# Dilated attention in a fused transformer kernel: the product with the values turned round, so that it leaves the array by features

## What is computed

```python
q, k, v = split(x @ w_in, 3)               # 48 heads of 64: 3 patterns x 16 heads
q, k = rope(rmsnorm(q)), rope(rmsnorm(k))
for g, (window, dilation) in enumerate(((128, 1), (512, 4), (2048, 16))):
    o[g], lse[g] = banded_softmax_attention(q[g], k[g], v[g])
wts = softmax(stack(lse), axis=0)          # over the three patterns
y = sum_g(wts[g] * o[g]) @ w_out           # 16 heads of 64 -> 1024
```

## Time and profile before

| | us |
|---|---|
| median of 3 runs (2498.86 to 2504.4) | 2503.65 |
| the profiled execution's own time | 2499.47 |
| its span | 2498.2 |
| PE busy (share of the span) | 2326.4 (93%) |
| DVE busy | 1221.8 (49%) |
| ACT busy | 969.2 (39%) |
| mean granted PE clock, share of full | 0.961 |

### The profile page before, as it was taken

The page is one execution under the profiler, slowest core; times in us unless marked ns, Lnnn a source line. Parts: engine busy times, 40 slices in busy tenths (PEclk is TensorE's granted clock), DMA queues, the critical chain, the costliest instruction groups (busy, mean ns, idle before and its releaser), DMA issues.

```text
span 2498.2 us, 37765 instructions
## 1 busy us (share of the span) xinstructions
PE 2326.4 (93%) x16663; PEld 2120.0 (85%) x16663; DVE 1221.8 (49%) x1521; ACT 969.2 (39%) x1145; POOL 506.6 (20%) x453
## 2 busy tenths in 40 slices
PE   6999999989999999889999899979999989888998
PEld 6998899979999998557999877867888877657997
DVE  5645566646555543445655345362122264545444
ACT  3433344434343433334444244333222233534442
POOL 2112434302111211220221101012202210230220
PEclk9999999989999999789999999989999999999999
DMA  6555433445555555666554310113332322213551
GB/s 242 175 173 173 139 122 133 136 169 174 182 179 185 180 182 173 229 237 236 172 183 155 124 35 18 34 68 101 101 98 88 102 96 85 68 51 93 181 183 68
DMA packets 205245, 344.72 MB, mean 138 GB/s; under 512 B 8845, under 2 KB 69498, under 8 KB 205082
## 3 DMA queue, kind: packets, MB, share of 16 engines
q1 hardware_dynamic: 205082, 342.31, 41.0%
HBM read 341.24 MB, written 1.05 MB: 137 GB/s over the span
## 4 chain that ended last, share of the span: by engine, by line
PE 80%; DVE 9%; POOL 4%; ACT 4%; issue 2%; SPq 0%; DMA 0%; DVEq 0%; POOLq 0%; ACTq 0%
PE PS L466 77%; PE PS L475 3%; DVE WL L452 2%; ACT WH L439 1%; POOL small L1454 1%; DVE rstd L587 1%; DVE XL L634 1%; POOL TMP L1463 1%; DVE XL L1002 0%; DVE al L998 0%; POOL small L1452 0%; DVE TMP L1382 0%; POOL TMP L1464 0%; DVE TMP L1387 0%; DVE al L1371 0%
## 5 line engine op out<-in xcount | busy, mean ns | idle before, releaser
L452 DVE TENSOR_TENSOR WL<-raw,WH 128x2048 fp32r<-128x2048 f32 (+2 forms) x281 | 651.6, 2331 | 720.7 <-ACT WH L439 720.7
L466 PE MATMUL PS<-XH,WH 128*128 128x256 f32 (+1 forms) x2336 | 699.3, 299 | 40.3 <-issue 15.3
L466 PE MATMUL PS<-XL,WH 128*128 128x256 f32 (+1 forms) x2336 | 692.9, 297 | 0.0
L466 PE MATMUL PS<-XH,WL 128*128 128x256 f32 (+1 forms) x2336 | 692.6, 297 | 0.0
L439 ACT ACTIVATE WH<-raw 128x2048 fp32r<-128x2048 f32 (+2 forms) x281 | 518.8, 1858 | 361.6 <-PE PS L466 361.1
L466 PEld LDWEIGHTS PS<-XH,WH 128*128 128x128 f32 x2336 | 451.6, 193 | 56.6 <-issue 18.5
L466 PEld LDWEIGHTS PS<-XL,WH 128*128 128x128 f32 x2336 | 452.6, 194 | 10.1
L466 PEld LDWEIGHTS PS<-XH,WL 128*128 128x128 f32 x2336 | 452.2, 194 | 10.0
L466 PE MATMUL PS<-WH,XH 128*128 128x256 f32 (+2 forms) x944 | 287.3, 304 | 17.3 <-DVE XL L634 8.5
L466 PE MATMUL PS<-WL,XH 128*128 128x256 f32 (+2 forms) x944 | 279.1, 296 | 0.0
L466 PE MATMUL PS<-WH,XL 128*128 128x256 f32 (+2 forms) x944 | 278.9, 295 | 0.0
(11 more groups left out here) (232 smaller groups left out, 2573.2 us busy)
## 6 DMA issues: line engine op xcount, KB each, us to landing
raw<-in_ffn_w_in SPq DMA_DIRECT2D x88, 1024.0 KB, 5.1
raw<-in_w_mod SPq DMA_DIRECT2D x48, 1024.0 KB, 5.2
raw<-in_ffn_w_out SPq DMA_DIRECT2D x40, 1024.0 KB, 4.9
raw<-in_a_w_in SPq DMA_DIRECT2D x36, 1024.0 KB, 4.9
raw<-in_w_mlp_in SPq DMA_DIRECT2D x32, 1024.0 KB, 5.5
raw<-in_w_mlp_out SPq DMA_DIRECT2D x32, 1024.0 KB, 5.0
raw<-in_gla_w_in SPq DMA_DIRECT2D x12, 1024.0 KB, 5.0
raw<-in_attn_w_qkv SPq DMA_DIRECT2D x6, 1024.0 KB, 5.0
```

The lines of the kernel that those rows point to most:

```text
L452: dve.e.tensor_tensor(self.WL[j % NRAW][:, 0:nk * nn], self.raw[j % NRAW][:, 0:nk * nn], wh.bitcast(F32), ALU.subtract).then_inc(*self.lo. ...
L466: return self.pe.e.matmul(out, l, r, start=start, stop=stop, skip_group_check=skip)
```

## The change

`pv` now takes two steps (the two heads of a pair, same token block) at once. The weights are 64 columns of values, in the left half of the array's columns for one head and in the right half for the other, their matmuls in turns, and what moves is the 128 columns of `aPT`. So bank 7 holds features on its partitions and tokens along the row. Both steps are done at even i. `turn_p` uses bank 5 or 6 for the first block only, and bank 3 (second half of an even step), 2 and 4 (odd step) for the rest. The inverse sums are taken at i = 7, behind the rotation, spread by ACT over 64 columns a head at the start of i = 8, and transposed on PE (`sums`, 4 transposes). ACT copies bank 7 out at the end of a group, and DVE multiplies the copy with the transposed inverses. The result is already by features: `turn_o` goes, and the split into `XH` and `XL` is done in four parts, three of them in group 3 at i = 1, 3, 5 and one at the end.

```diff
@@ attn_out_pe / attn_out_act / attn_out_dve
-        self.turn_o_pe(tag + "o", O, ready, 1)
+        if O is not None:
+            self.turn_o_pe(tag + "o", O, ready, 1)
...
-        self.turn_o_act(tag + "o", 1)
+        if tag == "lat":
+            self.turn_o_act(tag + "o", 1)
@@ new, per part g of the output
+        self.act.e.activation(self.XH[h][:, 2 * g:2 * g + 2, :], O, ACT.Copy).then_inc(*self.xh.up((tag, 2 * g)))
...
+        self.dve.e.tensor_tensor(self.XL[h][:, 2 * g:2 * g + 2, :], O, self.XH[h][:, 2 * g:2 * g + 2, :].bitcast(F32), ALU.subtract).then_inc(*self.xl.up((tag, 2 * g)))
@@ dilated_pe, turn_p
-                b = spare = 11 - spare
+                if u or c0:
+                    b = ((None, 3), (2, 4))[u][c0 // 3]
+                else:
+                    b = spare = 11 - spare
@@ dilated_pe, pv(hs, s0)
+            for s in (s0, s0 + 1):
                 pe.wait_ge(self.emptied, ("dil", "p", hs, s))
...
+                for s in (s0, s0 + 1):
+                    pair, j = divmod(hd, 2)
+                    m = self.mm(PS[64 * j:64 * j + 64, 7, pair * 256 + tb * 128:pair * 256 + tb * 128 + 128], self.aV[hb][:, g, kb * 256 + hd * 64:kb * 256 + hd * 64 + 64],
+                                self.aPT[s % 2][:, i * 128:i * 128 + 128], i == 0, i == 3 * nk - 1, True)
@@ dilated_pe
+        def sums(hs):
+            b = spare = 11 - spare
+            pe.wait_ge(self.evac, ("dil", "r", hs))
+            self.pe_bank(b)
...
+                    m = self.tr(PS[:, b, o:o + 128], self.aT[3][:, 256 * tb + 128 * pair:256 * tb + 128 * pair + 128])
@@ dilated_pe, main loop
                     turn_p(hs, i - 1)
-                    if i > 1:
-                        pv(hs, i - 2)
                     turn_p(hs, i)
                 if hs >= 0 and i in (2, 4, 6, 8):
                     pv(hs, i - 2)
                 if hs >= 0 and i == 8:
-                    pv(hs, 7)
+                    sums(hs)
@@ dilated_act, main loop
             for i in range(10):
+                if hs >= 0 and i == 8:
+                    act.wait_ge(self.v_step, ("dil", "recip", hs))
+                    act.e.activation(self.aT[3].rearrange("p (h d) -> p h d", d=64), self.small[:, 48:56].unsqueeze(2).to_broadcast([128, 8, 64]), ACT.Copy).then_inc(*self.evac.up(("dil", "r", hs)))
                 if hs + 1 < 4 and i < 9:
                     self.act_begin()
...
+                if hs == 3 and i in (1, 3, 5):
+                    split(i // 2)
+            if hs >= 0:
+                act.wait_ge(self.weighed, ("dil", hs, 7))
+                act.e.activation(self.aOT[:, 2 * hs:2 * hs + 2, :], PS[:, 7, :].rearrange("p (k t) -> p k t", k=2), ACT.Copy).then_inc(*self.evac.up(("dil", "o", hs)))
+        split(3)
@@ dilated_dve, main loop
+                if hs == 3 and i in (1, 3, 5):
+                    self.split_o_dve("dilo", i // 2, 1, self.aOT[:, i - 1:i + 1, :])
+                if hs >= 0 and i == 7:
+                    dve.wait_ge(self.expd, ("dil", hs, 7))
+                    dve.e.reciprocal(rd, den).then_inc(*self.v_step.up(("dil", "recip", hs)))
...
-            dve.wait_ge(self.weighed, ("dil", hs, 7))
-            dve.e.reciprocal(rd, den).then_inc(*self.v_step.up(("dil", "recip", hs)))
...
-                t = dve.e.tensor_tensor(dst[:, tb], PS[:, 7, tb * 256:tb * 256 + 256].rearrange("p (h d) -> p h d", h=4),
-                                        rd[:, 4 * tb:4 * tb + 4].unsqueeze(2).to_broadcast([128, 4, 64]), ALU.mult)
...
+            dve.e.tensor_tensor(self.aOT[:, 2 * hs:2 * hs + 2, :], self.aOT[:, 2 * hs:2 * hs + 2, :], two(PS[:, self.bank_of["dil", "r", hs], :]), ALU.mult).then_inc(*self.o_done.up(("dil", hs)))
```

More of the change, by code:

```diff
@@ L270, in phase_views @@
         self.aO = v(X0, 0, [128, 2048]).rearrange("p (b d) -> p b d", b=2)
+        self.aOT = self.tiles(v(X0, 0, [128, 2048]))
         self.aT = [v(X1, 512 * i, [128, 512]) for i in range(4)]
@@ L963, in x_free @@
         return {"dil": [(self.turned, ("residual", 0, 3)), (self.v_step, "tables")],
-                "f1": [(self.turned, ("dilo", "o", 3))],
+                "f1": [(self.xl, ("dilo", 5))],
                 "f2": [(self.lin, ("f1", "up", 5))],
@@ L1121, in turn_o_dve, with split_o_act, split_o_dve @@
             self.xl.name((tag, 2 * k2 + 1))
+    def split_o_act(self, tag, g, h, O, ready):
+        for signal, key in ready:
+            self.act.wait_ge(signal, key)
+        self.act.e.activation(self.XH[h][:, 2 * g:2 * g + 2, :], O, ACT.Copy).then_inc(*self.xh.up((tag, 2 * g)))
+    def split_o_dve(self, tag, g, h, O):
+        self.dve.wait_ge(self.xh, (tag, 2 * g))
+        self.dve.e.tensor_tensor(self.XL[h][:, 2 * g:2 * g + 2, :], O, self.XH[h][:, 2 * g:2 * g + 2, :].bitcast(F32), ALU.subtract).then_inc(*self.xl.up((tag, 2 * g)))
+        self.xl.name((tag, 2 * g + 1))
     def attn_out_pe(self, tag, O, ready, w_out):
-        self.turn_o_pe(tag + "o", O, ready, 1)
+        if O is not None:
+            self.turn_o_pe(tag + "o", O, ready, 1)
         for half in range(2):
@@ L1135, in attn_out_dve @@
     def attn_out_dve(self, tag, nxt, at):
-        self.turn_o_dve(tag + "o", 1)
+        if tag == "lat":
+            self.turn_o_dve(tag + "o", 1)
         for half in range(2):
@@ L1232, in turn_p, with pv @@
                 self.empties([b], (self.evac if c0 else self.emptied, ("dil", "p", hs, s)))
-        def pv(hs, s):
-            hd, tb, _ = self.dil_step(s)
-            u, hb = s % 2, hs % 2
+        def pv(hs, s0):
+            hb, tb = hs % 2, s0 // 2 % 2
             nk = tb + 1
-            for i in range(3 * nk):
-                o, kb = divmod(i, nk)
-                g = self.dil_order(s)[o]
+            if s0 == 0:
+                self.pe_bank(7)
+            for s in (s0, s0 + 1):
                 pe.wait_ge(self.emptied, ("dil", "p", hs, s))
@@ L1243, in pv @@
                     pe.wait_ge(self.evac, ("dil", "p", hs, s))
[L1244 to L1249, removed]
+            for i in range(3 * nk):
+                o, kb = divmod(i, nk)
+                for s in (s0, s0 + 1):
+                    hd, _, _ = self.dil_step(s)
+                    pair, j = divmod(hd, 2)
+                    g = self.dil_order(s)[o]
+                    pe.wait_ge(self.evac, ("dil", "v", hs, g))
+                    m = self.mm(PS[64 * j:64 * j + 64, 7, pair * 256 + tb * 128:pair * 256 + tb * 128 + 128], self.aV[hb][:, g, kb * 256 + hd * 64:kb * 256 + hd * 64 + 64],
+                                self.aPT[s % 2][:, i * 128:i * 128 + 128], i == 0, i == 3 * nk - 1, True)
+                    if i == 3 * nk - 1:
+                        m.then_inc(*self.weighed.up(("dil", hs, s)))
+        def sums(hs):
+            nonlocal spare
+            b = spare = 11 - spare
+            pe.wait_ge(self.evac, ("dil", "r", hs))
+            self.pe_bank(b)
+            for pair in range(2):
+                for tb in range(2):
+                    o = pair * 256 + tb * 128
+                    m = self.tr(PS[:, b, o:o + 128], self.aT[3][:, 256 * tb + 128 * pair:256 * tb + 128 * pair + 128])
+            m.then_inc(*self.turned.up(("dil", "r", hs)))
+            self.bank_of["dil", "r", hs] = b
+            self.empties([b], (self.o_done, ("dil", hs)))
         for hs in range(-1, 4):
@@ L1270, in dilated_pe @@
             if hs >= 0:
-                self.empties([7], (self.o_done, ("dil", hs)))
-        self.attn_out_pe("dil", self.aO, (self.o_done, ("dil", 3)), w_out)
+                self.empties([7], (self.evac, ("dil", "o", hs)))
+        self.attn_out_pe("dil", None, None, w_out)
     def dilated_act(self):
@@ L1321, in turn_p, with split @@
             act.e.activation(self.aPT[s % 2][:, 384:768], PS[:, b, 0:384], ACT.Copy).then_inc(*self.evac.up(("dil", "p", hs, s)))
+        def split(g):
+            self.split_o_act("dilo", g, 1, self.aOT[:, 2 * g:2 * g + 2, :], [(self.o_done, ("dil", g)), (self.lin, ("dil", 3, 8))])
         for hs in range(-1, 4):
             for i in range(10):
+                if hs >= 0 and i == 8:
+                    act.wait_ge(self.v_step, ("dil", "recip", hs))
+                    act.e.activation(self.aT[3].rearrange("p (h d) -> p h d", d=64), self.small[:, 48:56].unsqueeze(2).to_broadcast([128, 8, 64]), ACT.Copy).then_inc(*self.evac.up(("dil", "r", hs)))
                 if hs + 1 < 4 and i < 9:
@@ L1417, in dilated_dve @@
                     self.dve_mods.send(1)
+                if hs == 3 and i in (1, 3, 5):
[3 more added lines that the diff above has]
+                    dve.e.reciprocal(rd, den).then_inc(*self.v_step.up(("dil", "recip", hs)))
             if hs < 0:
                 continue
-            dve.wait_ge(self.weighed, ("dil", hs, 7))
-            dve.e.reciprocal(rd, den).then_inc(*self.v_step.up(("dil", "recip", hs)))
-            dst = self.aO[:, :, hs * 256:hs * 256 + 256].rearrange("p b (h d) -> p b h d", h=4)
-            dve.wait_ge(self.v_step, ("dil", "recip", hs))
```

(11 more changed lines are left out.)

## The result

| | before | after |
|---|---|---|
| median, 20 runs each (us) | 2498.86 | 2495.98 |
| lowest to highest | 2495.84 to 2504.52 | 2491.3 to 2497.77 |
| profiled execution: time, span | 2499.47, 2498.2 | 2491.8, 2490.2 |

The ratio is 0.9978, 95% interval 0.9971 to 0.9984. That is 5.5 us faster (4.0 to 7.2), where 11.6 us were forecast. The ratio takes in all runs and lies near that of the means (2494.9 to 2499.9 us), while the medians are only 2.9 us apart. The repeated runs of the changed kernel lie in two heaps, 7 of them at 2491.3 to 2492.0 and 13 at 2495.8 to 2497.8, without one between.

A forecast was written before the change was run, and what follows sets the result against it. PE was taken to bound the dilated stage, only just, with latency ruling group 3. Gains of 3.0 + 4.1 + 4.5 = 11.6 us gave 2487.9 for the profiled execution, 2492.0 for the median; range 2485 to 2499.

The forecast's parts named there:

- the end: Group 3 up to the output product: 6.5 us gained by an earlier start, less 2.0 for the clock, leaving 4.5.
- the period of 72.5 us: Sign to look for: groups 0 and 1 would each take about 72.5 us.
- The price of a pass: `pv` in column halves: 0.27 us a pair of four passes, 18 pairs 4.9 us, 3.0 less a group.
- (b): Rival: column halves in `pv` take turns, 0.116 us a pass; no gain in all, 2503.5 us; chance 0.12.
- (c): Rival: in `pv` one half's weights can't load while the other computes, 0.17 us a pass; 2520 us; chance 0.08.
- Banks: Groups -1 to 2: with five banks the two stalls before transposes go, 1.9 us a group; 0.4 may stay.
- The wait at i = 8: ACT waits for inverse sums behind DVE's rotation, delaying PE's `turn(9)` and next projection; 1.5 of PE's 4.4 us gained a group.
- The term of 1.5 us a group: Groups 0 and 1: next projection starts at 439.5 instead of 441.06, 3.0 us for both together.
- If PE runs ahead, these 2.4 us go and the rotation ends at 435.45: DVE's waits for PE's products between 397 and 438 us, 0.94 and 1.44, vanish; before, the rotation ended at 437.85.
- the forecast's 4.1: Group 2, no split rounding in the way: group 3's scores start at 511.7 instead of 515.79, 4.1 us.
- The term of 2.0 us for the clock: Output product now begins at 1.2 GHz, costing 2.0 us, between bounds of nothing and 2.9.
- Rival (a): The wait for inverse sums costs nothing; PE's 4.4 us count in three groups, 13.2, plus 6.5; 2484 us; chance 0.12.

The follow-up runs named there:

- the run that kept PE busy: Changed kernel plus 16 and 14 extra PE passes of 128x256, results unused, at i = 8 in groups 0 and 1; ratio 0.9964 to the kernel before.
- the early inverse: Changed kernel with the reciprocal at i = 7 moved from behind DVE's rotation to right behind `turn_p`; ratio 0.9942 to the kernel before.
- the spread copy late: Changed kernel with ACT's spread copy and its wait moved to the end of i = 8, the inverse left late; ratio 0.9939 to the kernel before.
- the remainder behind: Changed kernel with DVE's remainder of i = 7 moved behind the rotation and the inverse; ratio 0.9953 to the kernel before.
- the fill late: The early inverse with group 3's fourth modulation step of ACT and DVE moved from i = 6 to the end of i = 7; ratio 0.9920 to the kernel before.
- the spread copy first: The fill late with ACT's spread copy moved to i = 7, ahead of the fill's roundings; ratio 0.9920 to the kernel before.

## Why the prediction was right, and where it was off

The direction and the range held; the size was twice the measured one. Two things helped the range. The forecast of 2492.0 counted from 2503.65, the median of three runs; twenty give 2498.86, from which the same 11.6 us lead to 2487.3, 8.7 below what was measured. And the end gave 2.1 us more than forecast, against 6.9 less in groups 0 to 2. Of the signs named, the period of 72.5 us failed (75.3 and 75.2 in groups 0 and 1), and PE idled 3.7 us there at i = 8, not 2 to 3.

**The price of a pass.** 0.27 us a pair was taken, 0.245 measured (4 x 0.061). Rivals (b) and (c) fall. Two loads of 64 columns and two passes of 128 fit in 0.122 us, and in a list without turns a pass costs 0.099; so, by the start times, loads of one half go on while the other computes. Whether the passes of the two halves also run at once isn't shown. The rule of the Trainium skill (TensorE: Matmul & The Clock Gate, Part 3, The mechanism), that only another row group lets a weight load overlap, isn't borne out here. The background weight buffer, which the section names beside the row group, can't be told apart by these runs.

**Banks.** The two stalls went, as said. Alone the edit was worth 8.7 us rather than 3 times 1.9 (7.0 in groups 0 to 2 of its profile). A wait that the prediction didn't have came with the whole change: in groups 0 to 2 PE stands 0.7 us before one projection, for DVE's scaling (L1430).

**The wait at i = 8.** The mechanism was right, link by link, and so was the reading that PE's own 4.4 us a group couldn't all be had. The term of 1.5 us a group was wrong, for two reasons. First, "If PE runs ahead, these 2.4 us go and the rotation ends at 435.45" failed. DVE's waits did shrink, from 0.94 and 1.44 us to 0.00 and 0.30. But the head sums of projection 7, ready 1.8 us sooner, sent POOL's small step into DVE's remainder, which made it 2.35 us long instead of 0.20 and took the gain back. The last addition ended at 437.58, 0.3 us sooner than before. Moving the remainder showed it. The Trainium skill (SBUF — State Buffer, Who interferes with whom) says that DVE and GpSimd share one pair of ports as an exclusive lock; the trace agrees with 2.35 us, ending with DVE's instruction of 2.28, against 0.20. Second, the prediction counted the new idle as idle alone. It let the clock fall, 3.5 us for groups 0 and 1 by the run that kept PE busy; a part of that showed in group 2, whose time before its own i = 8 holds the 8.01 us projection. With PE kept busy group 2 gains 4.0 us on before, as the forecast's 4.1, and not 1.7.

**The end.** The product started right behind `pv` and `sums`, which came as reckoned: a stall of 5.7 us, then six pairs at half clock in 2.8 us where 3.0 were taken. The term of 2.0 us for the clock measured nothing: the clock came back at 549 us, as the product began.

```profile
546.22 2.83 PE L467 MATMUL PS<-al,al 128*64 128x128 f32 x24 [5.66 <-DVE al L1443]
548.98 0.78 PE L476 MATMUL PS<-CST,al 128*128 128x128 f32 x4
549.51 0.36 PE L467 MATMUL PS<-XH,WH 128*128 128x256 f32 x1
```

Rival (a), in which the wait cost nothing and 19.7 us were gained, was wrong for this change; the early inverse, which takes the wait away, gained 14.5.

## What to carry to other kernels

A new wait at the head of an engine's list costs what stands behind it, not what it waits for. Look for the earliest place where its input is ready and the latest where its output is due, and put both ends there. When an engine is made faster, check what its results now run into: a small step that hid in a gap may land beside a long instruction of another engine. And allow for a new idle of PE twice: once as idle, and once as the projection behind it, which may run at half clock.

## What the runs showed of the hardware

- The length of an idle alone didn't decide the clock here. Single idles of 1.93 us (the spread copy late), 1.61 (the remainder behind, group 1) and 2.50 us (the fill late) left it at 2.4 GHz. Nearly the same ones, 1.60 us (the remainder behind, group 0) and 2.48 us (the spread copy first), took it to 1.2 GHz, soon after PE was back at work.
- 1.94 and 1.72 us with four transposes between took it to 1.2 GHz for 6.8 us in group 1 of the changed kernel. In group 0 of the same profile the same pair cost less: the projection took 6.58 us instead of 8.01.
- The two heaps of runs, 4.5 us apart, would fit one or two such falls more or less. The runs at 2491 us had a mean clock of 0.960 to 0.962, those at 2496 us 0.956 to 0.960. Which falls they were no profile shows; the cause of the heaps stays open.
- 128x8 elements on POOL took 0.20 us alone and 2.35 us when begun beside a 128x2048 subtraction on DVE with both inputs in SBUF. In the early inverse the same subtraction met POOL's next step instead, which took 3.58 us in place of 1.64. In the kernel before this happened too, twice a group (381.74 and 398.37 us), at other projections.
- Column halves overlapped when their matmuls were neighbours in PE's list: 0.061 us a pass in turns, 0.099 with one half's matmuls all ahead of the other's.
